# Filter transform products in front of the last squares' sums, and three pieces of work dealt out anew

## The reference

```python
h = jnp.sin(z @ w1 + b1); h = jnp.sin(h @ w2 + b2)
h = (h @ w3 + b3).reshape(seq_len, HY_ORDER, 2, HY_WIDTH)
h = h * (jnp.exp(-t * jnp.abs(hy_decay)) + HY_MOD_SHIFT)      # window
h = h * lax.rsqrt(jnp.sum(h * h, axis=(0, 2), keepdims=True) + EPS)
# z = parts[n] * long_conv(z, h_pos, h_neg, bias)   for n in 0, 1   (rfft of the filter times rfft of z)
```

## Time and profile before

| | |
|---|---|
| median of 3 runs | 868.31 us (863.45 to 868.75) |
| profiled execution, own time | 864.98 us |
| its span, first to last instruction | 862.1 us |
| mean granted TensorE clock | 0.967 |
| busy share of the span: TensorE / VectorE / ScalarE | 90% / 49% / 33% |

### The profile page before, as it was taken

One profiled execution on the slowest core, in us unless ns is written; L12 is line 12 of the kernel. 1 busy time (PEld: TensorE's weight loads), 2 busy tenths in 40 slices (PEclk: granted clock), 3 DMA queues, 4 the chain that ended last, 5 costly groups with the idle time before them and its releaser, 6 DMA issues.

```text
span 862.1 us, 16880 instructions
## 1 busy us (share of the span) xinstructions
PE 778.7 (90%) x6727; PEld 448.2 (52%) x6727; DVE 419.9 (49%) x761; ACT 281.2 (33%) x559; POOL 108.5 (13%) x211
## 2 busy tenths in 40 slices
PE   4998799999999999999998999799999989899920
PEld 1232455554554457456664444357777667566610
DVE  5566713225881681754554675733343333243428
ACT  1667702113101201256222333223333333233315
POOL 4000100000001000001002000122222222122231
PEclk9999999999999999989999999799999999999975
DMA  8978451132044402133009516969999999999145
GB/s 246 411 300 341 134 195 36 63 114 82 18 178 165 132 1 99 25 123 123 0 22 367 202 44 221 397 244 418 416 420 416 419 418 420 419 415 393 61 150 233
DMA packets 40681, 191.40 MB, mean 222 GB/s; under 512 B 4641, under 2 KB 4937, under 8 KB 33010
## 3 DMA queue, kind: packets, MB, share of 16 engines
q1 hardware_dynamic: 29434, 155.12, 45.5%
q0 software_dynamic: 8640, 29.00, 9.9%
q10 hardware_dynamic: 2552, 6.50, 2.1%
HBM read 174.15 MB, written 16.45 MB: 221 GB/s over the span
## 4 chain that ended last, share of the span: by engine, by line
PE 73%; DMA 12%; DVE 7%; issue 3%; ACT 3%; SPq 1%; POOL 0%; POOLq 0%; DVEq 0%; ACTq 0%
PE banks L1654 16%; PE banks L2003 14%; DMA arena<-in_w_up 8%; PE banks L2014 6%; PE banks L1794 4%; PE banks L1655 4%; PE banks L1898 4%; PE banks L1888 4%; PE banks L1803 3%; DMA arena<-in_w_ada 3%; PE banks L1624 2%; PE banks L1686 2%; PE banks L1759 2%; PE banks L1558 2%; PE banks L1604 1%
## 5 line engine op out<-in xcount | busy, mean ns | idle before, releaser
L2003 PE MATMUL banks<-arena 128*32 128x256 f32 x3072 | 177.1, 382 | 9.0 <-DMA arena<-in_w_up 7.9
L1654 PE MATMUL banks<-arena 128*128 128x512 f32 x320 | 164.2, 595 | 1.5 <-issue 0.8
L2003 PEld LDWEIGHTS banks<-arena 128*32 128x32 f32 x3072 | 115.2, 111 | 63.0 <-issue 12.7
L1655 PEld LDWEIGHTS banks<-arena 128*128 128x128 f32 x320 | 60.8, 190 | 76.5 <-issue 76.5
L1480 DVE STREAM_TRANSPOSE arena<-arena 128x256 f32<-128x256 f32 x49 | 32.3, 659 | 135.3 <-PE banks L2003 130.1
L2014 PE MATMUL banks<-arena 128*32 128x256 f32 x1536 | 92.7, 379 | 1.2 <-DVE arena L1504 1.2
L2014 PEld LDWEIGHTS banks<-arena 128*32 128x32 f32 x1536 | 57.6, 110 | 26.7 <-DVE arena L1504 1.7
L1655 PE MATMUL banks<-arena 128*128 128x128 f32 x320 | 61.5, 274 | 0.0
L893 ACT ACTIVATE arena<-banks 32x256 f32<-32x256 f32 x98 | 36.7, 374 | 71.3 <-PE banks L2014 70.7
L1487 DVE COPY arena<-banks 32x256 f32<-32x256 f32 x98 | 41.4, 422 | 33.2 <-PE banks L2014 32.5
L1654 PEld LDWEIGHTS banks<-arena 128*128 128x128 f32 x320 | 48.5, 192 | 4.8 <-issue 3.3
(11 more groups left out here) (378 smaller groups left out, 985.5 us busy)
## 6 DMA issues: line engine op xcount, KB each, us to landing
arena<-in_w_down SPq DMA_DIRECT2D x16, 2048.0 KB, 31.1
arena<-in_w_gate SPq DMA_DIRECT2D x15, 2048.0 KB, 26.7
arena<-in_w_up SPq DMA_DIRECT2D x15, 2048.0 KB, 31.7
arena<-in_w_ada SPq DMA_DIRECT2D x12, 2048.0 KB, 13.6
arena<-in_w_in SPq DMA_DIRECT2D x7, 2048.0 KB, 7.7
expert_output<-arena ACTq DMA_DIRECT2D x49, 128.0 KB, 6.5
expert_output<-arena POOLq DMA_DIRECT2D x1, 4096.0 KB, 20.4
arena<-in_w_out SPq DMA_DIRECT2D x2, 2048.0 KB, 7.9
```

Of the source, the lines that this page charges most:

```text
L1654: M(ps[:, b, :], lhs, hT[:, k, CTX:TOK], start=k == 0, stop=k == KD - 1)
L1655: mm = M(ps[:, b + 1, 0:CTX], lhs, hT[:, k, 0:CTX], start=k == 0, stop=k == KD - 1)
L2003: mm = M(ps[q * LANE:(q + 1) * LANE, 2, 0:2 * P].rearrange("p (g a j) -> p g a j", g=2, j=LANE), xg[:, k, :], gate_up[e % 3][:, :, k, q, : ...
```

## The change

- TensorE: transform product g 0 starts when tile 1 is combined (`comb_done` 1), g 1 when tile 2 is (2), g 2 when all are (4); `combine` now signals for every tile but tile 0. The third batch of the squares' sums stands between g 1 and g 2, and the sums over the lanes (L1630) behind g 2 instead of g 0.
- ScalarE: it reads g 0 ahead of its wait for the squares' sums. In the second order it scales row tiles 0, 1 and 2 only (0 and 1 after g 4, 2 after g 5).
- VectorE: it scales row tiles 3 and 4, and makes `mod` and `scaleA`, ahead of its reading of g 7 in the second order. The two cosine instructions of the second order move behind its share of `hT`, ahead of the reciprocal of the norms (L1107); those of the first order stay where they are.
- TensorE's wait ahead of the transposes is for the three row tiles of ScalarE and for `modA_ready`, which VectorE gives behind the other two.

```diff
--- before.py
+++ after.py
@@ -661,10 +661,10 @@
                 win(w + 1)
             square(w)
             if w % 10 == 9:
+                spectrum(o, 0)
                 act.wait_ge(S["sq_done"], 3 * o + 3)
                 for i, rows in enumerate((P, 2 * LANE)):
                     link(A(lane_sums[i], ps[0:rows, 5 + i, :], ACT.Copy), "lanes_read")
-                spectrum(o, 0)
                 for t in ((0,), (2, 3))[o]:
                     x_square(t)
                 act.wait_ge(S["norm_done"], o + 1)
@@ -682,7 +682,7 @@
                     spectrum(o, g)
                     if o and g < 8:
                         act.wait_ge(S["xrs_ready"], 1)
-                        for t in {4: (0, 1, 2), 5: (3,), 6: (4,)}[g]:
+                        for t in {4: (0, 1), 5: (2,), 6: ()}[g]:
                             link(A(x_raw[:, t, :], x_raw[:, t, :], ACT.Copy, scale=xrs[:, t:t + 1]), "xn_ready")
             if w == 10:
                 ada_row(0)
@@ -958,12 +958,27 @@
         link(CP(gate_pick[:, :, 0:H], folded[:, 0:2, :]))
         link(CP(gate_pick[:, :, 32:32 + H], folded[:, 2:4, :]))
 
+        def ada_columns(third):
+
+            dve.wait_ge(S["ada_t"], third + 1)
+            lo = 16 * third
+            src = ps[:, ADA_BANK[third], :].rearrange("p (b j q) -> p j b q", b=4, j=4)[:, :, :, 0:2]
+            bias = colsT[:, lo:lo + 16].rearrange("p (j b) -> p j b", j=4).unsqueeze(3).broadcast_to((P, 4, 4, 2))
+            return link(TT(mod[:, lo:lo + 16, :].rearrange("p (j b) g -> p j b g", j=4), src, bias, ALU.add),
+                        "mod_ready")
+
         def combine(o, t):
 
             dve.wait_ge(S["sq_ready"], 10 * o + 2 * t + 2)
             link(TT(ab[:, 1, t, :], ab[:, 1, t, :], ab[:, 0, t, :], ALU.subtract))
             link(STT(ab[:, 0, t, :], ab[:, 0, t, :], 2.0, ab[:, 1, t, :], ALU.mult, ALU.add),
-                 "comb_done" if t == NT - 1 else "dve_chain")
+                 "comb_done" if t else "dve_chain")
+
+        def cosine_halves(o):
+
+            h = spec_h[:, o, 0]
+            link(TT(h[:, 0:4:2, :], h[:, 0:4:2, :], h[:, 1:4:2, :], ALU.add))
+            link(STT(h[:, 1:4:2, :], h[:, 1:4:2, :], -2.0, h[:, 0:4:2, :], ALU.mult, ALU.add))
 
         for o in range(ORD):
             for w in range(10):
@@ -992,6 +1007,12 @@
                 if o and g == 3:
                     dve.wait_ge(S["x_rstd"], 1)
                     link(dve.reciprocal(xrs, xss), "xrs_ready")
+                if o and g == 7:
+                    for t in (3, 4):
+                        link(TS(x_raw[:, t, :], x_raw[:, t, :], xrs[:, t:t + 1], None, ALU.mult))
+                    ada_columns(0)
+                    link(STT(scaleA, mod[:, 8:16, :], 1.0, colsT[:, 48:56].unsqueeze(2).broadcast_to((P, 8, 2)),
+                             ALU.add, ALU.mult), "modA_ready")
                 n = 20 * o + 10 + g
                 dve.wait_ge(S["filt_done"], n + 1)
                 dve.wait_ge(S["spec_read"], 6 * o + (4 if g == 7 else 1))
@@ -999,23 +1020,10 @@
                 old, total = {1: (3, 1), 2: (1, 0), 3: (3, 2), 7: (2, 0)}[g]
                 link(TT(h[:, total, :], h[:, old, :], new, ALU.add))
                 link(TT(h[:, old, :], new, h[:, old, :], ALU.subtract), "filt_read")
-            h = spec_h[:, o, 0]
-            link(TT(h[:, 0:4:2, :], h[:, 0:4:2, :], h[:, 1:4:2, :], ALU.add))
-            link(STT(h[:, 1:4:2, :], h[:, 1:4:2, :], -2.0, h[:, 0:4:2, :], ALU.mult, ALU.add))
-
-
-        def ada_columns(third):
-
-            dve.wait_ge(S["ada_t"], third + 1)
-            lo = 16 * third
-            src = ps[:, ADA_BANK[third], :].rearrange("p (b j q) -> p j b q", b=4, j=4)[:, :, :, 0:2]
-            bias = colsT[:, lo:lo + 16].rearrange("p (j b) -> p j b", j=4).unsqueeze(3).broadcast_to((P, 4, 4, 2))
-            return link(TT(mod[:, lo:lo + 16, :].rearrange("p (j b) g -> p j b g", j=4), src, bias, ALU.add),
-                        "mod_ready")
-
-        ada_columns(0)
-        link(STT(scaleA, mod[:, 8:16, :], 1.0, colsT[:, 48:56].unsqueeze(2).broadcast_to((P, 8, 2)),
-                 ALU.add, ALU.mult), "modA_ready")
+            if o == 0:
+                cosine_halves(o)
+
+
         for n in range(1, 10, 2):
             dve.wait_ge(S["xt_done"], n + 1)
             bank = 1 + n % 4
@@ -1103,6 +1111,7 @@
             link(TT(xc, p[0], p[1], ALU.add))
             link(TT(xs, p[2], p[3], ALU.subtract), "mul_done")
 
+        cosine_halves(1)
         dve.wait_ge(S["norm_cols"], 32)
         link(dve.reciprocal(norm_columns, norm_columns))
         for o in range(ORD):
@@ -1608,11 +1617,13 @@
                 piece = ((1, 3, 6, 9), (3, 6, 9))[o]
                 if w in piece:
                     ada_piece(4 * o + piece.index(w))
-            sum_squares(o, 2)
-            pe.wait_ge(S["comb_done"], o + 1)
             pe.wait_ge(S["ld_dft"], 32)
             for g in range(10):
                 n = 20 * o + 10 + g
+                if g == 2:
+                    sum_squares(o, 2)
+                if g < 3:
+                    pe.wait_ge(S["comb_done"], 4 * o + (1, 2, 4)[g])
                 b = filter_bank(n)
                 if g == 7:
                     pe.wait_ge(S["ab_ready"], o + 1)
@@ -1624,7 +1635,7 @@
                         mm = M(ps[:, b, :], dft_l[:, tb, part, f * P:(f + 1) * P], ab[:, part, 1 + tb, :],
                                start=tb == tbs[0], stop=tb == tbs[-1])
                 mm.then_inc(S["filt_done"], 1)
-                if g == 0:
+                if g == 2:
                     pe.wait_ge(S["lanes_read"], 2 * o + 2)
                     for i, rows in enumerate((P, 2 * LANE)):
                         mm = M(ps[0:1, 5 + i, :], lane_pick[0:rows, :], lane_sums[i], start=True, stop=True)
@@ -1635,7 +1646,8 @@
 
         pe.wait_ge(S["filt_read"], 28)
         pe.wait_ge(S["spec_read"], 12)
-        pe.wait_ge(S["xn_ready"], NT)
+        pe.wait_ge(S["xn_ready"], 3)
+        pe.wait_ge(S["modA_ready"], 1)
         for n in range(10):
             b = 1 + n % 4
             if n >= 4:
```

## The result

The changed kernel took 858.15 us (median of six executions, 855.54 to 859.18), the kernel before 865.93 in the same comparison (863.45 to 868.75). The ratio is 0.9902, 95% interval 0.9883 to 0.9921: 8.5 us faster, 6.8 to 10.1. The forecast was a gain of 4.85 us and a time of 861.8. The measured time lies in its range (856.5 to 866.5), and the gain of 0.98% still within 1%, but at its very edge, with an interval (0.9883 to 0.9921) that keeps clear of no change, and the gain is 1.75 times the one forecast. The profiled execution took 858.82 us, with a span of 856.2.

A forecast was written before the change was run, and what follows sets the result against it. TensorE, busy 90% of the span, was taken to bound the kernel. Gains of 0.64 us (first boundary) and 4.2 us (second boundary and rows) made 4.85, taken from 866.65 for 861.8 us; range 856.5 to 866.5.

The forecast's parts named there:

- First boundary: First-order filter section, last squares' sums to g 7: g 7 starts at 56.1 instead of 56.74, worth 0.64 us.
- the root's chain: First boundary: lane sums, table load, root, bias rows, reading of g 3; the root ends 0.86 us later, g 7 waits 1.0.
- Second boundary and rows: Second-order filter section through the turning of the rows: transposes 2.8 us earlier, then another 1.4 us, 4.2 together.
- the cover: VectorE's wait until 94.85 for ScalarE's reading of g 6 hides its two rows; at their upper price 0.35 us shows.
- 1.38 us of drain: Drain with ScalarE's table load at the first boundary: if still to come, a 0.7 us loss there instead of 0.64 gain.
- All that the change can remove of standing time: TensorE's waits at both boundaries and the turning of the rows: 2.75 + 2.75 + 2.09 + 2.09 + 1.02 = 10.7 us.
- Rival 1: Less low clock, at 0.77 from 535 to 565 us, adds 3.6 to 5.4 us: 857.3 us; chance 0.10.
- Rivals 2 to 4: Clock takes gain back, 870.9 us, chance 0.05; no gain at rows, 864.3, 0.08; time given back later, 866.65, 0.07.
- The bridge from the trace to the median: Whole kernel: starting time 866.65 us, halfway between the profiled 864.98 and the median 868.31.

The follow-up runs named there:

- the dealing alone: Kernel before with only two rows, modulation columns and `scaleA` moved to VectorE ahead of g 7 and second cosine halves behind the transposes; TensorE's order unchanged: ratio 0.9951.
- the variant: Changed kernel with VectorE reading g 3 ahead of its bias rows and the rows' root reciprocal between the bias instructions: mean 856.9 us over 10 executions.
- the order alone: Kernel before with only TensorE's new order, ScalarE reading g 0 ahead of its wait and `combine` signalling for every tile but tile 0: ratio 0.9962.

## Why the prediction was right in its section and wrong in its sum

- **The chain of each place was right.** First boundary 0.64 us: g 7 came at 56.15 for 56.1, with the root's chain last, as said. Second boundary and rows 4.2 us: 4.0 (102.58 against 107.16, less those 0.6), through transposes at 95.96 for 95.8. Their price on VectorE, 0.77 us, was near the 0.8 taken, and the cover held. The cosine instructions moved behind, the loads and the taps cost nothing that shows: 753.9 us behind the modulation pieces against 754.2.
- **The Trainium skill's 1.38 us of drain** beside the table load ("ScalarE: Activation LUTs", "What ACT_TABLE_LOAD costs") was rightly set aside: the root starts 1.30 us after the load in the new order too.
- **The step that failed is the first one:** "All that the change can remove of standing time is [...] 10.7 us". It priced a wait at its own length, from the one execution in which the clock stayed up. In four of the five traces of this kernel the clock falls behind those waits, and the products that follow take 1.4 to 1.6 us longer at a boundary, 4.6 in the worst. So the section cost 109.5 us on the mean and not 107.16. The term that the sum put at nothing, the clock lost behind the waits that the change removes, is 2.5 us by the five traces, all of it at the two boundaries (109.5 less 107.16 is 0.1 less, since the traces began by as much earlier on the mean), and with it the gain at the modulation pieces is 7.1 us, near the measured 7.5. I had written down 1.00 as the clock of the stretch and taken it for a property of the kernel.
- **Rival 1 had the right mechanism in the wrong place.** It let the clock give 3.6 to 5.4 us more, between 535 and 565 us, "for the change leaves that work as it is", at a chance of 0.10. What changed was the clock where the change was made. Rivals 2 to 4 didn't occur: behind the modulation pieces both kernels take the same time within 0.3 us on the mean.
- **The bridge from the trace to the median** added 1.4 us of error: it put the kernel before at 866.65, between a profiled 864.98 and a median of three, and 96 executions have a mean of 865.3. With the 2.7 us of gain left out, that makes the 4.1 us between the 861.8 forecast and the changed kernel's mean of 857.7; that the time lay inside the range is owed to the range's width of 10 us, not to the sum. The total of the profiled execution was an ordinary one and gave no hint of what was missing at the boundaries: behind the modulation pieces it took 754.9 us, the second longest of the five, and 2.9 us of its time lay outside the span.

What stays open is how large the clock's part is over many executions: five traces give 2.5 us with an error of 1.0, filling the waits gave back 1.7 (0.3 to 3.2) and 1.6 (0.3 to 2.9), and the timings put the excess at 2.7 to 2.9. That the clock falls behind these waits and stays up when they are filled doesn't hang on that: without filling, in the old order, it was low in 8 of 12 passes over a boundary (five traces of before, one of the dealing alone), with filling in none of 6. And the changed kernel still has 5.7 us of waits in these places (0.91, 0.98, 0.91, 1.08, 0.79 and 1.02 by the rows above). In the seven traces with the wait of 0.9 us ahead of g 2 (once 0.68; four of the changed kernel, two of the variant, one of the order alone) the clock never fell behind it, in 14 passes; whether by its length or by what stands around it wasn't tried.

## What to carry to other kernels

Take two or three traces of the kernel before, and look at the granted clock in windows of a few microseconds behind each wait of TensorE. If it is low in one of them, see whether the work behind comes later for it: then the wait costs more than it lasts, and a change that fills it can gain more than its length; where another wait behind it shrinks by as much, as at the transposes here, it costs nothing. An ordinary total of the profiled execution doesn't show that its rows are ordinary too.

## What the runs showed of the hardware

- Behind two waits of 1.62 and 1.13 us with 1.06 us of products between them the clock fell to 1.2 GHz in part of the executions (in six of the ten passes over a boundary in the five traces), after TensorE had been busy for 27 of the 31 us ahead of the first boundary and 32 or more of the 35 us from 45 to 80. The same kernel in the same place kept 2.4 GHz in other executions.
- One product of 128x512 in each of these waits kept the clock up at both boundaries in all three traces that have them, and the kernel got faster by work that nobody reads: 0.9980 (0.9963 to 0.9997).
- A multiply of 128x1024 fp32 from and to SBUF with a scalar per partition took 0.77 us on VectorE, where such rows took 1.17 on ScalarE (each as one of several in a row).
- 24 transposes of 128x128 fp32 took 2.84 us with the clock up and 4.76 with it partly at 1.2 GHz.
